# Moving a 64-byte scale tile in front of the two weight tiles of a transformer kernel

## The reference

```python
proj = h @ w_in[l]                                    # 1024 -> 9,792 columns
x = x + gate1 * (merged @ w_o[l])
ff = jnp.square(jax.nn.relu(h2 @ w_mlp1[l])) @ w_mlp2[l]
...
proj = jnp.einsum('bsd,de->bse', u, w_in[l])          # 1024 -> 3072
h = h + jnp.einsum('bsf,fd->bsd', jax.nn.silu(gate) * up, w_down[l])
```

## Time and profile before

| | |
|---|---|
| runs | 942.56, 955.08, 960.68 us |
| median | 955.08 us |
| the profiled execution's own time | 956.73 us |
| its span, first to last instruction | 954.9 us |
| TensorE clock granted, mean | 0.989 |
| matmuls in the trace | 7536, and as many weight loads |

### The profile page before, as it was taken

How to read it: one execution, slowest core, us unless ns; L and a number is a source line. 1 busy time by engine, 2 the same in 40 slices (tenths; PEclk the granted TensorE clock), 3 DMA queues, 4 the chain that set the end, 5 groups by cost and what they waited for, 6 DMA issues and landing times.

```text
span 954.9 us, 18288 instructions
## 1 busy us (share of the span) xinstructions
PE 922.9 (97%) x7536; PEld 885.3 (93%) x7536; DVE 666.7 (70%) x915; ACT 506.0 (53%) x686; POOL 92.0 (10%) x66
## 2 busy tenths in 40 slices
PE   4999999899989999999999999999998999999998
PEld 4799999789867889999999999999997999999998
DVE  6764999988478998786966544544786666666642
ACT  2485655666587684345555444345567554444331
POOL 0000255100335432000000000000000000000000
PEclk9898999999999999999999999999999999999999
DMA  9664444666412226664865555545331345555650
GB/s 377 255 234 158 164 161 162 222 232 213 172 61 73 89 89 221 226 244 171 272 212 178 184 199 191 177 139 193 133 133 45 133 138 195 197 176 178 222 195 23
DMA packets 25085, 168.01 MB, mean 176 GB/s; under 512 B 2868, under 2 KB 4532, under 8 KB 5048
## 3 DMA queue, kind: packets, MB, share of 16 engines
q1 hardware_dynamic: 23760, 164.90, 49.5%
q10 hardware_dynamic: 1256, 2.12, 0.6%
HBM read 165.95 MB, written 1.06 MB: 175 GB/s over the span
## 4 chain that ended last, share of the span: by engine, by line
PE 86%; DVE 5%; ACT 5%; DMA 2%; issue 2%; SPq 0%; DVEq 0%; ACTq 0%
PE bank L1788 85%; DVE acc L1103 2%; DMA adas<-w_stream 1%; ACT whi L568 1%; DVE wlo L1061 1%; PE bank L2039 1%; DVE cvt L1258 1%; DMA raw<-w_stream 1%; ACT kw__111 L787 0%; DVE kw__111 L1365 0%; ACT zt L812 0%; PE bank L2063 0%; ACT sp L878 0%; ACT sp L884 0%; ACT sp L876 0%
## 5 line engine op out<-in xcount | busy, mean ns | idle before, releaser
L1788 PE MATMUL bank<-hhi,whi 128*128 128x256 f32 (+1 forms) x1364 | 390.7, 288 | 0.1
L1788 PE MATMUL bank<-hhi,wlo 128*128 128x256 f32 (+1 forms) x1352 | 379.0, 280 | 0.0
L1788 PE MATMUL bank<-hlo,whi 128*128 128x256 f32 (+1 forms) x1352 | 378.9, 280 | 0.0
L1061 DVE TENSOR_TENSOR wlo<-raw,whi 128x2048 fp32r<-128x2048 f32 (+1 forms) x131 | 300.4, 2293 | 111.7 <-ACT whi L568 109.4
L568 ACT ACTIVATE whi<-raw 128x2048 fp32r<-128x2048 f32 (+1 forms) x132 | 250.4, 1897 | 97.4 <-PE bank L1788 75.9
L1788 PEld LDWEIGHTS bank<-hhi,whi 128*128 128x128 f32 (+1 forms) x1364 | 257.8, 190 | 6.7 <-issue 5.7
L1788 PEld LDWEIGHTS bank<-hlo,whi 128*128 128x128 f32 (+1 forms) x1352 | 256.9, 190 | 1.0 <-issue 0.6
L1788 PEld LDWEIGHTS bank<-hhi,wlo 128*128 128x128 f32 (+1 forms) x1352 | 256.6, 190 | 0.0
L1788 PE MATMUL bank<-fhi,whi 128*128 128x256 f32 x432 | 121.4, 281 | 0.0
L1788 PE MATMUL bank<-flo,whi 128*128 128x256 f32 x432 | 121.4, 281 | 0.0
L1788 PE MATMUL bank<-fhi,wlo 128*128 128x256 f32 x432 | 121.4, 281 | 0.0
(11 more groups left out here) (288 smaller groups left out, 1356.9 us busy)
## 6 DMA issues: line engine op xcount, KB each, us to landing
raw<-w_stream SPq DMA_DIRECT2D x147, 1024.0 KB, 4.9
adas<-w_stream SPq DMA_DIRECT2D x8, 1024.0 KB, 8.8
xres<-x_t SPq DMA_DIRECT2D x1, 1024.0 KB, 10.4
out<-oute SPq DMA_DIRECT2D x8, 128.0 KB, 3.8
tabs<-tabs_in_dram ACTq DMA_DIRECT2D x1, 641.0 KB, 4.1
tabs<-tabs_in_dram ACTq DMA_DIRECT2D x1, 512.0 KB, 3.8
hankel<-bucket_rows ACTq DMA_DIRECT2D x1, 512.0 KB, 5.8
cols<-cols_in_dram ACTq DMA_DIRECT2D x1, 325.0 KB, 8.3
```

The source lines that it names most:

```text
L1061: nc.vector.tensor_tensor(out=wlo[:, c % RING, 0:n], in0=raw[:, r % RING, 0:n], in1=whi[:, c % RING, 0:n].bitcast(f32), op=ALU.subtract)\
L1788: return nc.tensor.matmul(out, lhsT, rhs, start=start, stop=stop)
```

## The change

`mscale` is placed right behind `raw`. In the new layout it begins at 25728, `whi` at 25792 and `wlo` at 50368. `csil` and `mod`, which lie between `wlo` and the old place of `mscale`, begin 64 bytes higher too, at 74944 and 74976. `root` and everything behind it, and `raw`, keep their addresses. No instruction, wait, DMA or size is altered.

```diff
     raw = place("raw", [P, RING, CW], f32)
+    mscale = place("mscale", [P, 2 * KD], f32)
     whi = place("whi", [P, RING, CW], f32r)
     wlo = place("wlo", [P, RING, CW], f32r)
     csil = place("csil", [P, KD], f32)
     mod = place("mod", [P, 48], f32)
-    mscale = place("mscale", [P, 2 * KD], f32)
     root = place("root", [P, NT], f32)
```

## The result

The changed kernel took 972.04, 968.91, 971.67 and 968.66 us, median 970.29. The kernel before, with one more run beside it, has a median of 953.71 us. The ratio is 1.0218, with a 95% interval of 1.0163 to 1.0273. The change made the kernel slower, by 1.7% on the medians and 2.2% by the ratio; the interval holds 2%, so whether the loss is over 2% stays open. That it is a loss is clear: in the 46 further runs of the kernel before, beside the experiments, the highest was 963.06 us, and the lowest after the change is 968.66. The four runs also lie closer together: 3.4 us from the fastest to the slowest, against 18 before.

A forecast was written before the change was run, and what follows sets the result against it. The prediction took PE's matmuls on the split weights as the bound. Its four parts summed to 0 + 0 + 0 + 0 against the profiled 956.7 us; it forecast the runs' median, 955 us, range 935 to 967.

The forecast's parts named there:

- the two paces and their rhythm: PE's load and matmul streams: two stable rhythms, 113.3 and 117.8 ns a matmul, entered by the last interruption's timing.
- The mix: PE's triples: 4,400 matmuls at the long pace, 1,890 at the short; all short 937.3 us, all long 965.0 us.
- Parts 1 to 3: ACT writing `whi` (0 to 37 ns a chunk), DVE writing `wlo` (0 to 19 ns), scalar operands; each taken as 0.
- Part 4: PE loading weights from 64 modulo 128: bounded at 27.7 us slower or faster, taken as 0.
- Loads at 64 are no slower than 112 ns: Reason for 0: `adas` loads at the new residue, with one-column matmuls, came every 112 ns.
- The delayed load: Reason for 0: in PE's triple, the 192 ns load changes from `wlo` to `whi` between stretches with addresses unchanged.
- One with a shorter period: Reason for 0: a clash of period under 512 bytes is swept through inside each matmul; 64 bytes only shift its time.
- B: Each PE weight load touches one more 128-byte stretch, delaying every matmul by 4.4 ns: 984 us, chance 0.11.
- What would make me wrong: PE's two streams: a clash needing equal residues, invisible in a trace where they always differ by 64; no size given.
- A: The new residue decides PE's rhythm, nearly all short (937 us) or all long (965 us): chance 0.14.
- C: Equal residues of PE's weight and moving streams remove the cost down to 112 ns a matmul: 929 us, chance 0.09.

The follow-up runs named there:

- experiment 1: PE alone, weight and moving tiles shifted in 32-byte steps: 113.3 or 117.8 ns at distance (weight start minus moving start, modulo 256) 64, 118.6 or 120.0 at 128.
- experiment 9: Kernel before, with 128 bytes of small tiles placed between `whi` and `wlo`, so `wlo` begins 128 bytes higher and `whi` stays: 942.85 us, ratio 0.9906.
- experiment 4: Kernel before, with `mscale` between `wlo` and `csil`, so `csil` and `mod` move 64 bytes and the weight tiles stay: 951.66 us, ratio 0.995.
- Experiment 11: PE alone, moving operands of 32 to 256 columns at distances 64, 128 and 0: 111.7 ns a matmul up to 224 columns.
- experiment 5: PE alone, weights moved in 8-byte steps, and six settings moving only the lo activation or `wlo`: paces between 113.3 and 121.9 ns.
- all64: Kernel before, with every tile beginning 64 bytes higher, weights and moving operands together: 957.86 us, ratio 1.009.
- rest64: Kernel before, with 64 bytes left free before `hhi`, so all moving operands begin 64 bytes higher and the weights stay: 976.32 us, ratio 1.023.
- wlo128: Same run as experiment 9: kernel before, with `wlo` 128 bytes higher and `whi` in place: 942.85 us, ratio 0.9906.
- rest96: Kernel before, with 96 bytes left free before `hhi`, so the moving operands move and the weights stay: 960.51 us, ratio 1.008.
- small: Same run as experiment 4: kernel before, with only `mscale`, `csil` and `mod` moved: 951.66 us, ratio 0.995.
- rest128: Kernel before, with 128 bytes left free before `hhi`, so the moving operands move and the weights stay: 959.76 us, ratio 1.012.
- wlo64: Kernel before, with `mscale` between `whi` and `wlo`, so `wlo`, `csil` and `mod` begin 64 bytes higher and `whi` stays: 965.30 us, ratio 1.013.

## Why the prediction was wrong

The forecast was 955 us, in a range of 935 to 967; the kernel took 970.29.

**What bounds the kernel, the two paces and their rhythm** were read rightly. 113.3 and 117.8 ns are two rhythms of one and the same address setting, and PE alone produces both in experiment 1. The mix was sized well too: of the uninterrupted triples before, 1,427 are near 353 ns and 532 near 340, that is 4,281 and 1,596 matmuls where I took 4,400 and 1,890. "This mix is enough to explain a spread as wide as theirs" has the support of experiment 9: with only one rhythm left the spread of 11 runs is 8.5 us, against 20 for the 16 runs beside it.

**Parts 1 to 3** held: 1911 against 1907 ns for ACT, 2317 against 2306 for DVE, 752 against 752 and 474 against 476 for the scalars (DVE's subtraction is just above the 2.29 to 2.31 us that I gave for it), and experiment 4 shows no loss for the small tiles.

**Part 4 is the step that failed: "I take 0, for three reasons from rows."** The term measured +15.5 us, 2.5 ns on each matmul of the triples (119.1 against 116.6 ns on the mean), because at distance 128 the two streams have rhythms of 118.7 and 120.0 ns and no longer those of 113.3 and 117.8. The reasons, one by one:

- "Loads at 64 are no slower than 112 ns" is true and beside the point. Experiment 11 has 111.7 ns for loads at any distance, so long as the moving operand is shorter. I took a bound on one of the two streams for a bound on the pair.
- "The delayed load goes from `wlo` to `whi` ... with the addresses unchanged." This shows that a rhythm has more than one phase. I took it to mean that the addresses play no part, where they set which rhythms there are. What picks one of these isn't shown; groups of one setting differed in nothing but what had run before them.
- "One with a shorter period is swept through inside every matmul ... a shift by 64 would only move the time within the matmul at which it comes." The first half stands: the period, 256, isn't longer than 512, and the step of `kb` is without effect. The second half fails. It treats a clash as a fixed toll, the same wherever it falls, and a shift of 64 bytes did change the pace. Experiment 11 shows that the same two streams lose nothing with 224 columns and some 2 to 8 ns with 256. I read this as a delay whose cost depends on where in the matmul it comes and on whether there is slack behind it. That the streams delay each other at some relative positions, and that a delay shifts the position of the next one, would give both the jagged dependence of experiment 5 and the separate rhythms. This mechanism is argued and not shown; shown is that the distance sets the paces.

The Trainium skill's "SBUF — State Buffer", section "Who interferes with whom", calls PE's two read ports independent and says that PE never waits on anyone. The prediction took from it that the weight address is worth 0 us, and this isn't borne out: with PE alone at work, what the pair costs depends on the difference of the two start addresses, 113.3 to 121.9 ns. Whether the two reads delay each other at the ports or elsewhere, no run shows.

**The rivals.** B had the right sign, but not its mechanism or its price. A load that touches one more stretch of 128 bytes would make all64 slow and leave rest64 alone; they did the reverse. Its price, one unit of 4.4 ns on each matmul, 27.7 us, was nearly twice the 15.5 measured, since the new paces, 118.7 and 120.0, lie 0.9 and 2.2 ns above the long one of before, and 5.4 and 6.7 above the short one. Its sign in the profile, loads of 192 ns or more at all three places and a pace of 122 ns, came half true: 190 ns at all three places, and 120.0 ns. "What would make me wrong is a clash between the streams that needs equal residues to arise at all" is near to what happened, and I gave it no chance of its own. A had the addresses decide between two known rhythms; there are others. C's floor of 112 ns for each matmul was reached by no setting with 256 columns: 113.3 was the least.

## What to carry to other kernels

When the matmul stream is the bound, and each matmul of 256 columns has its own 128x128 weight load in fp32r, the difference between the start addresses of the two tiles is a tuning parameter worth some per cent (942.85 to 976.32 us here), and so is whatever is allocated between them. Other shapes and formats weren't run, but for narrower moving operands, which lost nothing. Read the pace from starts in unbroken stretches, try a few placements in a small kernel of PE alone, and repeat each several times, since one placement can have two or three paces. A spread between runs of one program was itself a sign here: two paces at the same addresses in one trace came from a pair of streams that is sensitive to their distance.

## What the runs showed of the hardware

- Triples of 128x128 loads and 128x256 moving operands in fp32r ran at 113.3 to 121.9 ns for one matmul at the 2.4 GHz level, depending on the distance modulo 256 bytes. 113.3 and 120.0 ns are 136 and 144 periods of 1.2 GHz. The commonest paces between, 115.6, 116.7, 117.8, 118.3 and 118.7 ns, lie 1/3, 1/2, 2/3, 3/4 and 4/5 of the way from the one to the other, and at 118.7 the starts repeat every five matmuls. This looks like whole steps of 8 periods that some matmuls of a round lose and others don't; it is arithmetic on the measured means, and no run shows what the step is.
- The dependence is there with all other engines idle, begins between 224 and 256 columns, and isn't altered by steps of 512 and 1024 bytes.
- In whole kernels, the matmuls counted in 120.1 us from 500 us on were 1060 (`wlo128`), 1030 (`rest96`), 1020 (before, `all64`, `small`, `rest128`), 1016 (`wlo64`) and 1001 (after, `rest64`). The median times run from 942.85 to 976.32 us in nearly the same order.
- Loads with a moving operand of 32 to 224 columns came every 111.7 ns. The Trainium skill, "TensorE: Matmul & The Clock Gate", section "LDWEIGHTS (loading the stationary operand)", gives columns / 1.2 for a load, by which 128 columns take an estimated 106.7 ns; the rows show 5 ns more in a stream.
